# Merge, experts and combination in one program part, expert blocks unrolled with the down products one block late

## What is computed

```python
# merge: h = rms_norm(x + (gate_s * ssm(u) + gate_a * attn) @ w_out)
g_sel = argmax(h @ w_router_group)                 # 1 of 4 groups
top_v, top_i = top_k(expert logits of that group, 2)
w_assign = softmax(top_v) * g_w                    # two weights per token
# each expert (32 of them, D_EXPERT = 512):
#   e = (silu(h @ w_gate) * (h @ w_up)) @ w_down
# combination: y = rms_norm(x2 + w_0 * e_0 + w_1 * e_1) * g_final
```

## Time and profile before

| | |
|---|---|
| median of 3 runs | 1308.66 us (1303.22 to 1314.2) |
| profiled execution, its own time | 1310.04 us |
| span of its trace | 1308.4 us |
| mean granted TensorE clock | 0.881 |
| TensorE matmul busy | 1076.5 us (82%) |
| VectorE busy | 409.1 us (31%) |
| ScalarE busy | 328.0 us (25%) |
| GpSimd busy | 276.0 us (21%) |
| DMA moved | 299.36 MB, mean 229 GB/s |

### The profile page before, as it was taken

How to read it: one execution, slowest core, us unless ns; L and a number is a source line. 1 busy time by engine, 2 the same in 40 slices (tenths; PEclk the granted TensorE clock), 3 DMA queues, 4 the chain that set the end, 5 groups by cost and what they waited for, 6 DMA issues and landing times. The chain is left out here.

```text
span 1308.4 us, 18689 instructions
## 1 busy us (share of the span) xinstructions
PE 1076.5 (82%) x6695; PEld 679.5 (52%) x6695; DVE 409.1 (31%) x890; ACT 328.0 (25%) x666; POOL 276.0 (21%) x673
## 2 busy tenths in 40 slices
PE   5999999789977868899997288888888888878750
PEld 5999998566655646677444233333333333333320
DVE  4456347647734553414212600000000100000006
ACT  6422222446622231210012022222221222212212
POOL 0006940588721100000000112121111111111110
PEclk9999999879968878989999599788887888898985
DMA  8322252430056517400401779999999999999916
GB/s 335 128 90 73 92 194 88 137 113 1 6 183 185 179 36 315 173 1 1 153 33 57 297 296 410 403 405 406 410 410 403 408 403 407 401 401 412 409 68 232
DMA packets 75132, 299.36 MB, mean 229 GB/s; under 512 B 12630, under 2 KB 35030, under 8 KB 48566
## 3 DMA queue, kind: packets, MB, share of 16 engines
q1 hardware_dynamic: 65934, 280.16, 55.3%
q0 software_dynamic: 7984, 17.33, 4.0%
q10 hardware_dynamic: 1152, 1.05, 0.2%
HBM read 284.26 MB, written 25.58 MB: 237 GB/s over the span
## 5 line engine op out<-in xcount | busy, mean ns | idle before, releaser
L2082 PE MATMUL ps<-arena,local_experts 128*64 128x512 f32 x1024 | 230.0, 598 | 11.4 <-DMA arena<-in_w_exp 10.5
L353 PE MATMUL ps<-local_project 128*128 128x288 f32 (+4 forms) x1608 | 205.9, 290 | 15.2 <-DVE local_project L491 11.6
L353 PEld LDWEIGHTS ps<-local_project 128*128 128x128 f32 (+1 forms) x1608 | 204.7, 184 | 16.0 <-DVE local_project L392 11.6
L2099 PE MATMUL ps<-arena,local_experts 128*64 128x512 f32 x512 | 166.6, 810 | 21.3 <-ACT local_experts L2121 21.3
L2139 DVE SCALAR_TENSOR_TENSOR local_experts<-local_experts,ps 64x512 f32<-64x512 f32 x32 | 21.7, 679 | 464.4 <-ACT local_experts L2117 464.4
L2082 PEld LDWEIGHTS ps<-arena,local_experts 128*64 128x64 f32 x1024 | 83.1, 138 | 155.4 <-issue 155.4
L2099 PEld LDWEIGHTS ps<-arena,local_experts 128*64 128x64 f32 x512 | 52.6, 184 | 108.7 <-issue 108.7
L2061 PE MATMUL ps<-arena,local_experts 64*128 64x64 f32 x457 | 49.4, 246 | 53.1 <-DVE local_experts L2142 42.5
L2047 POOL TENSOR_TENSOR local_experts<-local_experts 1x1 f32<-1x1 f32 x32 | 5.9, 185 | 391.8 <-ACT local_experts L2126 391.8
L2061 PEld LDWEIGHTS ps<-arena,local_experts 64*128 64x128 f32 x457 | 40.1, 162 | 83.7 <-DVE local_experts L2142 46.9
L2126 ACT ACTIVATE local_experts<-ps 64x512 f32<-64x512 f32 x64 | 37.9, 593 | 178.2 <-PE ps L2099 177.4
(11 more groups left out here) (390 smaller groups left out, 1416.7 us busy)
## 6 DMA issues: line engine op xcount, KB each, us to landing
arena<-in_w_exp SPq DMA_DIRECT2D x192, 1024.0 KB, 20.5
arena<-in_w_rest SPq DMA_DIRECT2D x9, 1024.0 KB, 5.7
local_attention<-in_cache SPq DMA_DIRECT2D x56, 128.0 KB, 2.7
arena<-in_w_wide SPq DMA_DIRECT2D x6, 1040.0 KB, 5.0
arena<-scratch_sig SPq DMA_DIRECT2D x2, 2304.0 KB, 14.0
arena<-in_x SPq DMA_DIRECT2D x2, 2048.0 KB, 11.6
arena<-in_cache SPq DMA_DIRECT2D x32, 128.0 KB, 2.3
arena<-in_cache POOLq DMA_DIRECT2D x32, 128.0 KB, 3.6
```

The lines of the kernel that those rows point to most:

```text
L353: mm = pe.matmul(out, stationary(s, k), moving(m, k), start=k == 0 and a == 0, stop=k == KD - 1 and a == 2)
L2082: mm = pe.matmul(c.ps[SLOTS * u:SLOTS * (u + 1), 2 + u, :], XT[:, 4 * half + k], raw[at + 2 * half + u][:, k], start=half == 0 and k == 0, ...
L2099: mm = pe.matmul(c.ps[SLOTS * h:SLOTS * (h + 1), 6 + h, :], HT[:, k], raw[at + 4 + h][:, k], start=k == 0, stop=k == KE - 1)
```

## The change

- `merge`, `experts` and `combine` no longer open blocks of their own. Each returns its engine lists, and a new function `tail` puts them one behind the other in one block. The semaphore clears and the barriers between the three are gone.
- The ring of 12 places becomes three sets of six, `c.sets`, 18 places. The added places lie over `w1` and over `w_glu`, `w_ssm` and what follows them. SyncE fills one at the start of `merge`, two behind `attn_ps`, five behind `proj_ps` (with `x` loaded behind `attn_ps` now), eight behind the last matmul of the output projection (`out_ps`), one behind the last `h_ready`, and the last behind `blocks_ready`.
- The store of the last tile of `h` is issued by GpSimd, and so are the first two gathers, straight from `c.table`. VectorE writes `c.table` ahead of the block numbers instead of behind them, and signals `table_ready` and `blocks_ready`.
- The first 30 blocks are written out; the last ones stay in a hardware loop from pair 15 (two blocks here).
- In the unrolled blocks GpSimd uses the table directly as its index list, so two small copies and two small multiplications (`tick`) per block go. The two empty scatters ahead of the loop go too.
- TensorE's order per block is new, and so is the release of the places: `gu_used` for gate and up, `down_used` for down. Gate and up alternate between two pairs of PSUM banks.
- `combine` issues `g_final` first, then waits for `y_stored` itself.

The core of the diff:

```diff
 TensorE, block b (unrolled form)
+        transpose_rows(0, 16)
+        for b in range(FIXED):
+            q = b % 2
+            pe.wait_ge(xt_ready, b + 1)
+            gate_up(q, 0, *fixed_set(b))
+            if b >= 1:
+                turn_hidden(b)
+            gate_up(q, 1, *fixed_set(b))
+            transpose_rows(1 - q, (b + 1) // 2 * 16 + 16)
+            if b == 1:
+                pe.wait_ge(c.table_ready, 1)
+            if b >= 2:
+                pe.wait_ge(y_out, 2 * (b - 1))
+            if b >= 1:
+                down(*fixed_set(b - 1), b)
 ...
+        turn_hidden(last * 2 + 2)
+        pe.wait_ge(y_out, last * 4 + 2)
+        down(IN_LOOP[1], fill * 16, last * 2 + 2)
 GpSimd
-            with pool.Fori(0, n) as i:
-                for q in range(2):
-                    pool.wait_ge(xt_ps, i * 2 + q + 1 + XT0)
-                    pool.tensor_copy(token[:, q], ...).then_inc(idx_copied, 1)
-                    pool.wait_ge(idx_copied, i * 4 + 2 * q + 2)
-                    pool.tensor_tensor(tick[:, 1 + q:2 + q], ...).then_inc(turn, 1)
-                    gather(q)
-                    pool.wait_ge(y_stored[q], i * 16 + STORED0)
-                    pool.tensor_copy(dest[:, q], ...).then_inc(idx_copied, 1)
-                    pool.wait_ge(idx_copied, i * 4 + 2 * q + 3)
-                    pool.wait_ge(y_out, i * 4 + 2 * q + 2 + Y0)
-                    pool.tensor_tensor(tick[:, 3 + q:4 + q], ...).then_inc(store_turn, 1)
-                    scatter(q, dest[:, q])
+        for b in range(FIXED):
+            pool.wait_ge(xt_ps, b + 1)
+            gather(b % 2, c.table[:, b + 2, 0:1])
+            pool.wait_ge(y_out, 2 * b + 2)
+            scatter(b % 2, c.table[:, b, 1:2])
 ScalarE
+        rows(1)
+        for b in range(FIXED):
+            if b >= 1:
+                hidden(b)
+            gates(b % 2, 4 * b + 4)
+            rows(b + 2)
+            if b >= 1:
+                result((b - 1) % 2, 2 * b, (b - 1) // 2 * 16 if b >= 3 else None)
 SyncE
+        for b in range(AHEAD, FIXED + 1):
+            if b < FIXED:
+                gate_up(b % AHEAD, lambda p: c.d["w_exp"][b, p], 4 * (b - AHEAD))
+            if b > AHEAD:
+                down((b - 1) % AHEAD, lambda p: c.d["w_exp"][b - 1, p], 2 * (b - 1 - AHEAD))
 merge, SyncE
-            sp.wait_ge(first_in, 16 * RING)
+        piece(0, 0)
+        sp.wait_ge(attn_ps, 16)
 ...
+        piece(0, 1)
+        piece(0, 2)
+        sp.wait_ge(proj_ps, 16)
+        for s, p in ((0, 3), (0, 4), (0, 5), (1, 0), (1, 1)):
+            piece(s, p)
 ...
+        sp.wait_ge(out_ps, 2 * TILES)
+        for s, p in ((1, 2), (1, 3), (1, 4), (1, 5), (2, 0), (2, 1), (2, 2), (2, 3)):
+            piece(s, p)
+        sp.wait_ge(h_ready, TILES)
+        piece(2, 4)
+        sp.wait_ge(c.table_ready, 1)
+        sp.wait_ge(c.blocks_ready, 1)
+        piece(2, 5)
 build
-        for phase in (project, ssm_build, prompt, sample, merge, experts, combine):
+        for phase in (project, ssm_build, prompt, sample, tail):
```

More of the change, by code:

```diff
@@ L1557, in merge @@
 def merge(nc, c):
-    with ExitStack() as ctx:
[L1561 to L1620, removed]
@@ new lines, in sem @@
+    def sem(name):
+        return c.sem("merge_" + name)
+    local = c.tail_local
+    region = Region(local, 0, LOCAL)
+    small = Region(c.arena, AT_Z4 + 16 * TOK, AT_KT)
+    sig = Region(c.arena, AT_Z4, AT_SSM).take([P, 16, TOK])
+    w_out = Region(c.arena, AT_KT, AT_XM).take([P, KD, D])
+    late = Region(local, 0, 3072)
+    w_glu = region.take([P, 4, D])
+    w_ssm = region.take([P, 4, D])
+    c.x2 = x = Region(c.arena, AT_XM, AT_X2_END).take([P, TILES, D])
+    h = late.take([P, 2, D])
@@ new lines, in merge @@
+    hT = late.take([P, KD, P])
+    w_attn = Region(c.arena, AT_X2_END, AT_LOCAL).take([P, 4, D])
+    glu = Region(local, region.pos, LOCAL).take([P, 4, TOK])
+    y = region.take([NCH, CH, SW])
+    route = Region(local, 13312, LOCAL)
+    tmp = region.take([P, 2, 2, 512])
+    yT = region.take([P, 4, TOK])
+    g_ffn = small.take([P, D])
+    w_route = small.take([P, KD, 36])
+    b_route = small.take([P, 36])
+    c.X_rows = small.take([SLOTS, 2, D])
+    c.table = small.take([SLOTS, TABLE, 2], I32)
@@ new lines, in merge @@
+    c.blocks = small.take([1, BLOCKS + 3], I32)
+    c.token = small.take([SLOTS, 2, 1], I32)
+    at_z = Region(c.arena, AT_Z4, AT_Z4 + 5 * 2048)
+    at_out = Region(c.arena, AT_KT, AT_XM)
+    at_attn = Region(c.arena, AT_X2_END, AT_LOCAL)
+    at_glu = Region(local, 3072, 3072 + 6 * 2048)
+    over_z = [at_z.take([P, 4, 512]) for _ in range(5)]
+    over_out = [at_out.take([P, 4, 512]) for _ in range(4)]
+    over_attn = [at_attn.take([P, 4, 512]) for _ in range(2)]
+    over_glu = [at_glu.take([P, 4, 512]) for _ in range(6)]
@@ L1641, in _ @@
[L1641 to L1649, removed]
-            sp.wait_ge(first_in, 16 * RING)
+            merge_sync(sp)
@@ L1652, in _ @@
+            n = experts_sync(sp)
+            combine_sync(sp, n)
+        @block.gpsimd
+        def _(pool):
+            merge_gpsimd(pool)
+            experts_gpsimd(pool)
         @block.tensor
         def _(pe):
[L1654 to L1663, removed]
@@ L1749, in _ @@
[L1749 to L1757 removed]
+            merge_tensor(pe)
```

1105 lines of the change are left out of this document (603 added, 502 removed).

## The result

The forecast was 1294.5 us, faster, with a range of 1266 to 1318. The changed kernel takes 1337.3 us (median of 4 runs, 1335.6 to 1339.6) against 1308.8 us of the kernel before beside it: ratio 1.024, interval 1.020 to 1.027. It is 28.5 us **slower**, outside the range and on the other side.

What follows compares the result with a forecast made beforehand. It took TensorE first, transfers at the end, as the bound. Start +0.1, periods -5.4 (30 x 16.1 + 5.0 against 493.4), last down products -0.5 and end -8.2 sum to -14.0 us: 1294.5 us from a median of 1308.66, range 1266 to 1318.

Steps and rivals of the forecast that it cites:

- the ring: Experts: down products, result copies, scatter, gather, transposes, next down products; period P 14.9 us plus clock 1.2, 16.1; chance 0.5.
- What bounds before: Experts of the kernel before: bound by both, TensorE first and transfers at the end; 15.92 us a block, transfers need 16.25.
- Start: Start of the experts: first gather 6.0 us earlier, used up by down products one block late; price +0.1 us.
- The new wait: TensorE, before each block's eight transposes: waits 2.7 us for the gathered rows, in place of the old waits.
- Gather's start: GpSimd, counted from a down start: copies end 4.90, scatter starts 5.5, gather starts at 6.75 us.
- Landing: Gather's rows land 7.2 us after its start; 0.7 later if GpSimd's queue is served in order, P = 15.6, untested.
- Clock: TensorE's down products: fallen clock adds 1.2 us a block, between 0 and 2.05.
- The rival on the slower side: Experts: the clock falls in each block, P = 16.95, 1320 us; chance 0.18, two thirds of it over 1% slower.
- The transfer-bound rival: Experts: if the clock doesn't fall, transfers bind, for P below 15.25; -40.7 us, so 1268; chance 0.22.
- The waits only move: Experts: gather isn't late, yet fallen clock keeps TensorE at 15.92 us a block; -19 us, so 1289; chance 0.1.
- Edits at nothing: Early places in `merge`, unrolled code and the store of h's last tile on GpSimd's queue: taken at no cost.
- End: Last scatter to `combine`'s row loads: 7.1 us of clears and barrier go but for 0.1, `g_final` 1.2; together -8.2.

Runs made afterwards that it cites:

- the run of before with its clock at 1.00: Kernel before, plus four 128x256 matmuls on TensorE ahead of its wait for the hidden values; 1305.3 us, ratio 0.998 to the kernel before.
- the gather first: Changed kernel, with the gather of block b+3 issued ahead of the scatter of block b in GpSimd's unrolled list; 1279.4 us, ratio 0.979 to the kernel before.
- the kernel with the two swapped: Changed kernel, gather still held until the earlier block's result is copied, but issued ahead of the scatter; 1275.4 us, ratio 0.975 to the kernel before.

## Why the prediction was wrong, point by point

**The step that failed.** It is the ring's period, P = 16.1 us in the sum, where 17.48 was measured. The path was right. Two terms of P were too small: the clock, 1.2 us where the runs show 1.85, and the gather's landing, 7.2 where they show 7.87. At 30 turns that alone takes the forecast from 1% faster to 2% slower.

**What bounds before: partly wrong.** "TensorE first, transfers at the end" is right as a reading of the waits, which begin for weights at 1121.82. But it took a busy TensorE at a fallen clock for something that the time depends on, and the run of before with its clock at 1.00 moved it by 3 us. The rows had it: a DMA share of 1.01 from 760 on the earlier trace rows. Over all 31 periods, the 15.92 us are the transfers' 16.25 less what the twelve places filled ahead gave.

**Start: right.** The table comes at 739.55 and the first gather starts behind it; the forecast for block 0's down products was 766.0, measured 765.72. Being one block late does use up the 6 us of the barrier. The timeline, to set beside the earlier trace rows:

```profile
739.55 0.26 DVE L1977 TENSOR_SCALAR arena<-ps 64x104 int32<-64x104 f32 x1 [2.28 <-PE ps L1788]
740.75 0.99 POOL L1683 DMA_INDIRECT arena<-scratch_h,arena  x1 [28.24 <-DVE arena L1977]
...
751.83 3.76 SPq L2047 DMA_DIRECT2D arena<-in_w_exp  x3
```

**The new wait: right in place, wrong in size.** It was named with its line, its cause and all that stands behind it; forecast 2.7 us a block, measured 3.64. This is no different mechanism but the ring with its terms mis-sized:

- *Gather's start* after the down products, 6.75 forecast, 6.96 at the full clock. The scatter starts 0.8 us behind the copies, not 0.6. +0.21.
- *Landing*, 7.2 forecast. Here the median is 8.0 (7.5 to 9.1) from 780 to 1220 us, partly outside the 6.2 to 7.8 that the prediction allowed, and the mean of all 30 turns is 7.87. The gather follows the scatter at 1.23 us and not 1.94. The prediction had this case at 15.6 and set it aside as "untested". +0.67. Against it, the transposes and the switch take 0.80 at the full clock and not 0.95: -0.15.
- *Clock*, 1.2 forecast, 17.48 - 15.63 = 1.85 measured. It was put "a little above the middle" of 0 and 2.05, with two hopes: that a longer period meets the fall less often and that the gate products hide some. In the turn shown the down products take 1.70 us longer than at 2.4 GHz, and all of it goes into the ring. +0.65. The row that the prediction gave for what TensorE did before the clock fell, 776.44 to 779.84, is from a block whose down products took 3.66 us, so the clock had not fallen there. That such a stretch is the cause is shown by the two runs with matmuls in it.

Together 17.48 - 16.1 = 1.38, by 30 blocks 41.4 us. With the start (-0.3), the last down products (+0.7) and the end (-1.7, below) that makes 40.1 of the 40.3. These four stretches make up the whole span, so the sum has to close, and the 0.2 is rounding. The general formula, 30P - 497, gives +27.4 for 17.48, and the measurement +28.5.

The Trainium skill's page TensorE: Matmul & The Clock Gate (HAM oscillation — how this bites in real kernels) says that waits between bursts of matmuls throttle the engine again each time. The trace agrees for 27 of the 31 down products of blocks 0 to 30, which took 4.7 us or more in place of 3.65, and not for the other four. The runs agree too: 0.89 granted without matmuls in the gap, 0.99 with them. The same clock of 0.89 has two prices here, 47 us in the changed kernel and 3 us in the kernel before.

**The rival on the slower side: right, with a wrong argument against it.** "The clock falls in each block" gave 1320. Against it stood "above 16.25 the DMA has idle time, and gathers land sooner then". The DMA did have idle time, 365 GB/s, and weights landed in 9 us and not 21.2, but gathers landed in 8.0 and not 7.2. Only behind 1210 us, with the transfers down to 182 to 332 GB/s, did they land sooner, in 5.8 in the median of six. That sentence was the only reason for a chance of 0.18, and no row carried it.

**The range: too narrow on the slower side.** The slower end held the clock's upper price (16.95) or the queue's (15.6), but not both. Nothing excludes one by the other. Both give 15.6 + 2.05 = 17.65, 30 x 17.65 - 497 = +32.5, or 1341. That case was worked out in its parts and left out as a sum.

**The transfer-bound rival: right as a kernel, wrong as a forecast.** It needs P below 15.25, and the ring stood 0.4 above that even without clock loss. With the gather first it came true.

**The waits only move: wrong.** The gather was late in each of the 30 turns, by 3.64 us in the mean.

**Edits at nothing: nothing in the runs is against it.** The table is written at 739.55 us, at 740.80 before, so `merge` didn't grow with the early loads. The unrolled code, with the gather first, runs at 11.95 us a block against 12.1 of TensorE's own work. In the closed ring weights are never waited for, so the early places can't have shortened it; with the ring open they are worth 15 to 16 us.

**End: right within 2 us.** From the last down products' start to the end of the span it was 1308.4 - 1259.28 = 49.1 us and is 1334.7 - 1295.95 = 38.8, so -10.4 against -8.7 (-8.2 and -0.5) forecast; the row loads follow the last scatter without barrier. The last down products start at 1295.95, 5.7 us after block 30's (5.0 forecast: they waited 1.48 us for ScalarE's copy of the turned hidden values, which the step left out). The timeline, beside the earlier trace rows:

```profile
1295.95 0.61 PE L2143 MATMUL ps<-arena 128*64 128x512 f32 x1 [1.48 <-ACT arena L2189]
...
1301.76 0.95 POOL L2079 DMA_INDIRECT scratch_rows<-local_tail,arena  x1 [0.55 <-issue]
...
1304.96 5.44 SPq L2262 DMA_DIRECT2D arena<-scratch_rows  x10
```

## What to carry to other kernels

When a result is moved one step late, go down each in-order list that holds an instruction waiting for it, and ask who waits for what stands behind: here a gather behind a scatter, and the order of the two decides between 2.4% slower and 2.5% faster. Once a ring is closed, each of its terms counts fully in each turn, the clock too, which costs almost nothing where transfers bind; unknown terms that point the same way belong into the range as their sum. To learn which of two full resources binds, ask what the time would be if the one were free: busy share and clock don't tell.

## What the hardware showed that was not expected

**Two indirect DMAs on GpSimd's queue behave as one after the other.** The second of a pair lands 9.1 to 9.2 us after the first one's start in the three kernels below, whichever of the two it is and whether it follows at 1.23 or at 1.94 us. Medians from issue to landing, 780 to 1220 us: gathers, then scatters of the changed kernel (gather second), then gathers and scatters of the kernel with the two swapped (scatter second).

```profile
DMA to landing us min/median/max: 7.5/8.0/9.1
DMA to landing us min/median/max: 6.1/7.2/7.7
```

```profile
DMA to landing us min/median/max: 6.7/7.3/8.2
DMA to landing us min/median/max: 7.2/7.9/9.1
```

Before: 1.94 + 7.2 = 9.14. Changed: 1.23 + 8.0 = 9.23. Swapped: 1.24 + 7.9 = 9.14 for the scatter, while the gather, now first, is at 7.3. Issuing the gather 0.7 us sooner behind a scatter gained nothing. Issuing it first did. That a queue served in order is the reason is the simplest reading, and not shown by itself. That the landing doesn't depend on the weights' depth is measured: behind a scatter, gathers land in 8.0 us with weights landing in 9 (changed kernel), and in 8.1 with weights landing in 29.8 (gather first).

**A few small matmuls hold the clock.** Six (changed kernel) or four (before) of 128x256 in a gap of 3 to 4 us took the granted clock from 0.89 to 0.99 and 1.00, where the small 64-column transposes that stand there alone leave it at 0.89. It is not held in every turn: in four of the 30 turns of the run with six of them, the down products still took 4.7 to 5.4 us.
